# Stick-breaking attention: the second head's high parts rounded on ScalarE, both heads' weights computed back to back

## The reference, cut to what matters

```
def stick_breaking_attention(q, k, v):
...
        z = jnp.einsum('bthd,bshd->bhts', qt, k).astype(jnp.float32) * scale
        strict = s_idx[None, :] < t[:, None]
        log_beta = jax.nn.log_sigmoid(z)
        log_1mb = jnp.where(strict, log_beta - z, 0.0)
        after = lax.cumsum(log_1mb, axis=3, reverse=True) - log_1mb
        a = jnp.where(strict, jnp.exp(log_beta + after), 0.0)
        o = jnp.einsum('bhts,bshd->bthd', a.astype(v.dtype), v)
```

## Time and profile before

| what | value |
|---|---|
| runs | 658.02 us median, 657.94 to 658.09 |
| profiled execution | 658.28 us, span 656.5 us from first to last instruction |
| granted TensorE clock, mean | 0.999 |
| TensorE busy | 647.1 us, 99% of the span |
| VectorE, ScalarE, GpSimd busy | 460.2, 384.4, 163.6 us |
| chain that ended last | TensorE 93%, ScalarE 2%, VectorE 2%, GpSimd 1% |

### The profile page before, as it was taken

One profiled execution on the slowest core, in us unless ns is written; L12 is line 12 of the kernel. 1 busy time (PEld: TensorE's weight loads), 2 busy tenths in 40 slices (PEclk: granted clock), 3 DMA queues, 4 the chain that ended last, 5 costly groups with the idle time before them and its releaser, 6 DMA issues.

```text
span 656.5 us, 9977 instructions
## 1 busy us (share of the span) xinstructions
PE 647.1 (99%) x3574; PEld 539.6 (82%) x3574; DVE 460.2 (70%) x627; ACT 384.4 (59%) x561; POOL 163.6 (25%) x123
## 2 busy tenths in 40 slices
PE   9999999999999999999999999999999999999996
PEld 6888887577888888888887888777888888888885
DVE  6498766877697878786457646676678788886532
ACT  7556355866757667666345435665567676767330
POOL 0323300001053434441001000680123434343000
PEclk9999999999999999999999999999999999999999
DMA  9887633004356363637652663304255444544601
GB/s 351 335 302 282 226 129 129 1 6 189 132 199 245 136 247 128 246 138 283 231 192 73 250 249 135 129 1 189 100 182 202 180 204 165 219 147 182 247 1 64
DMA packets 18971, 115.60 MB, mean 176 GB/s; under 512 B 2911, under 2 KB 3453, under 8 KB 6013
## 3 DMA queue, kind: packets, MB, share of 16 engines
q1 hardware_dynamic: 17789, 111.52, 45.4%
q10 hardware_dynamic: 1152, 3.67, 1.6%
HBM read 114.14 MB, written 1.05 MB: 175 GB/s over the span
## 4 chain that ended last, share of the span: by engine, by line
PE 93%; ACT 2%; DVE 2%; issue 1%; POOL 1%; DVEq 0%; POOLq 0%; ACTq 0%
PE ps L1422 27%; PE ps L1429 14%; PE ps L1379 11%; PE ps L1380 11%; PE ps L1381 11%; PE ps L1451 5%; PE ps L1506 2%; PE ps L1750 1%; PE ps L1634 1%; PE ps L1370 1%; PE ps L1678 1%; PE ps L1900 1%; PE ps L1884 1%; PE ps L1600 1%; POOL sb_splo L1351 1%
## 5 line engine op out<-in xcount | busy, mean ns | idle before, releaser
L777 DVE TENSOR_TENSOR wlo<-raw,whi 128x2048 fp32r<-128x2048 f32 x99 | 226.9, 2323 | 72.8 <-ACT whi L413 72.7
L413 ACT CAST whi<-raw 128x2048 fp32r<-128x2048 f32 x99 | 185.8, 1917 | 48.8 <-PE ps L1381 42.0
L1422 PE MATMUL ps<-xpair,whi 128*128 128x512 f32 x768 | 183.3, 391 | 0.0
L1422 PEld LDWEIGHTS ps<-xpair,whi 128*128 128x128 f32 x768 | 141.2, 188 | 27.6
L1429 PEld LDWEIGHTS ps<-xpair,wlo 128*128 128x128 f32 x768 | 98.5, 191 | 3.7
L1429 PE MATMUL ps<-xpair,wlo 128*128 128x256 f32 x768 | 99.6, 283 | 0.0
L1327 POOL TENSOR_TENSOR hidf<-act_g,conv 128x512 f32<-128x512 f32 x22 | 76.0, 3455 | 85.1 <-ACT act_g L671 85.1
L1379 PE MATMUL ps<-whi,hid_hi 128*128 128x512 f32 x176 | 68.5, 389 | 0.0
L1380 PE MATMUL ps<-wlo,hid_hi 128*128 128x512 f32 x176 | 68.5, 389 | 0.0
L1381 PE MATMUL ps<-whi,hid_lo 128*128 128x512 f32 x176 | 68.5, 389 | 0.0
L1379 PE MATMUL ps<-whi,xpair 128*128 128x512 f32 x168 | 67.7, 403 | 0.1
(11 more groups left out here) (197 smaller groups left out, 789.0 us busy)
## 6 DMA issues: line engine op xcount, KB each, us to landing
raw<-in_weights SPq DMA_DIRECT2D x101, 1024.0 KB, 4.9
c_gpost<-in_gpost ACTq DMA_DIRECT2D x4, 512.0 KB, 5.7
raw<-in_weights SPq DMA_DIRECT2D x3, 512.0 KB, 6.6
c_gpre<-in_gpre ACTq DMA_DIRECT2D x3, 512.0 KB, 4.3
h<-in_x SPq DMA_DIRECT2D x2, 512.0 KB, 3.9
out<-h SPq DMA_DIRECT2D x4, 256.0 KB, 2.0
raw<-in_weights SPq DMA_DIRECT2D x2, 256.0 KB, 4.7
t<-in_masks SPq DMA_DIRECT2D x1, 512.0 KB, 12.0
```

Source lines behind the costliest of these rows:

```text
L413: act.copy(whi[:, slot, :], raw[:, slot, :]).then_inc(hi_done, 1)
L777: dve.tensor_tensor(wlo[:, slot, :], raw[:, slot, :], whi[:, slot, :].bitcast(F32), ALU.subtract).then_inc(lo_done, 1)
L1422: pe.matmul(ps[:, b0 + m, :], whi[:, slot, cols], xpair[:, kt].rearrange("p a c -> p (a c)"), start=kt == 0, stop=kt == KT - 1, skip_group ...
```

## The change

On ScalarE the two W of a pair now stand together, in front of both E. The rounding of the second head's softplus is taken from GpSimd and becomes a copy on ScalarE (`sb_second_hi`), behind the E and in front of the L; for pair 0 it stands at the end of the work beside unit 5. GpSimd keeps the first head's rounding and both low parts; its low part of the second head waits for the new semaphore `sb_sph1`. VectorE and TensorE keep their lists.

```
-        sb_z, sb_absd, sb_exp1, sb_ln, sb_spd, sb_sph, sb_spl, sb_cum, sb_prob, sb_pv, sb_ohi, sb_olo = (
-            sem("sb_" + s) for s in ("z", "absd", "exp1", "ln", "spd", "sph", "spl", "cum", "prob", "pv", "ohi", "olo"))
+        sb_z, sb_absd, sb_exp1, sb_ln, sb_spd, sb_sph, sb_sph1, sb_spl, sb_cum, sb_prob, sb_pv, sb_ohi, sb_olo = (
+            sem("sb_" + s) for s in ("z", "absd", "exp1", "ln", "spd", "sph", "sph1", "spl", "cum", "prob", "pv", "ohi", "olo"))
...
+            def sb_second_hi(n):
+                act.wait_ge(sb_spd, 2 * n + 2)
+                if n >= 2:
+                    act.wait_ge(sb_cum, 2 * (n - 2) + 2)
+                act.copy(sb_sphi[:, n % 2, 1], sb_sp[:, n % 3, 1]).then_inc(sb_sph1, 1)
+
...
                             for hd in range(2):
                                 sb_log(1, hd)
+                            sb_second_hi(0)
...
             for n in range(NP):
                 for hd in range(2):
                     sb_weights(n, hd)
-                    if n + 2 < NP:
+                if n + 2 < NP:
+                    for hd in range(2):
                         sb_exp(n + 2, hd)
                 if n == 0:
                     act.wait_ge(unit_used, ODD_END["unit", 5])
                     act.copy(vbuf[:, :, BLK:2 * BLK], ps[:, 6:8, :]).then_inc(in_free_act, 1)
+                if n + 1 < NP:
+                    sb_second_hi(n + 1)
                 if n + 2 < NP:
                     for hd in range(2):
                         sb_log(n + 2, hd)
...
-                pool.tensor_copy(sb_sphi[:, n % 2, hd], sb_sp[:, n % 3, hd]).then_inc(sb_sph, 1)
-                pool.wait_ge(sb_sph, 2 * n + hd + 1)
+                if hd == 0:
+                    pool.tensor_copy(sb_sphi[:, n % 2, hd], sb_sp[:, n % 3, hd]).then_inc(sb_sph, 1)
+                    pool.wait_ge(sb_sph, n + 1)
+                else:
+                    pool.wait_ge(sb_sph1, n + 1)
                 pool.tensor_tensor(sb_splo[:, n % 2, hd], sb_sp[:, n % 3, hd], sb_sphi[:, n % 2, hd].bitcast(F32),
                                    ALU.subtract).then_inc(sb_spl, 1)
```

## The result

The changed kernel takes 660.70 us (median of 6 runs, 660.52 to 660.94), the kernel before, run beside it, 658.15 us (6 runs, 657.94 to 658.26). The ratio is 1.0039, 95% interval [1.0029, 1.0049]: 2.6 us slower (1.9 to 3.2). The forecast was slower, 660.2 us, range 659.1 to 661.4. The profiled execution took 660.61 us with a span of 658.8 us, against 658.28 and 656.5 us before.

What follows compares the result with a forecast made beforehand. A second way through ScalarE's copy and GpSimd's low part was to set a 3.74 us period, not TensorE's 3.08; 2.2 us lost on 658.28 gives 660.5, less 0.26 for the median: 660.2 us, range 659.1 to 661.4.

Steps and rivals of the forecast that it cites:

- The way and its pieces: Loop from W(n, 1) through ScalarE's copy, GpSimd's low part and TensorE's sums to W(n+1, 1): 3.74 us a pair.
- three places to the copy: ScalarE's steps through W, E, E to the copy, 0.37 to 0.42 us each: 1.20 us.
- the hand-over to GpSimd: From the end of ScalarE's copy to the start of GpSimd's low part of head 1: 0.08 us.
- The first pairs: Start of the stick-breaking stage: W(1, 1) at 424.13 against 423.97 before, entering the periods 0.16 us late.
- The 0.2 us that the prediction put to this: By the VectorE and GpSimd port lock rule, the split and low(0, 1) end earlier: 0.2 us off the sum.
- The sum: Five periods of 3.74 us from W(1, 1) to W(6, 1): head 1's sums of pair 6 come 2.2 us late.
- the last step: Stage's last step, no E left: the second way is 2.94 us, TensorE's 3.48 us bounds, nothing more is lost.
- the last step of the sum: From the profiled execution, 660.5 us, to the median of runs, 0.26 us lower: 660.2 us.
- hidden second way: Rival: low part done before head 1's sums need it, TensorE's 3.08 us sets the period: 656.5 us; chance 0.08.
- the neutral case: Rival: second way about as long as the present period, 3.30 to 3.45 us, no change: 658.0 us; chance 0.12.
- The clock: Rival: TensorE's idle time drops its clock to the lower level in this stage: 668 us; chance 0.02.
- ScalarE's added work does not count: ScalarE's busy time with eight more copies: 2.87 us of the 3.74 us period, so it does not fall behind.

Runs made afterwards that it cites:

- the reorder alone: Kernel before the change, with both W of a pair put before both E and all roundings kept on GpSimd: 657.61 us, ratio 0.9994.
- the spare copy: Both W before both E, GpSimd keeping all roundings, plus ScalarE's copy at the change's place into a tile nobody reads: 658.81 us, ratio 1.0007 to the kernel before.
- copy-first kernel: Changed kernel with the copy for the next pair directly behind the two W, in front of the E: 657.34 us, ratio 0.9985 to the kernel before.

## Why the prediction was right

**The way and its pieces.** It named the way that would set the period and priced it at 3.74 us; it measured 3.82. Piece by piece: three places to the copy 1.20, measured 432.62 - 431.41 = 1.21; the copy 0.52, measured 0.50; ScalarE to GpSimd 0.08, measured 0.17; the low part 1.00, measured 1.01; GpSimd to TensorE 0.05, the same; the products 0.79, the same; TensorE to ScalarE 0.10, measured 0.09. The one mis-sized term is the hand-over to GpSimd, taken from a place where GpSimd waits for one semaphore only, while the new low part waits for three; with one wait it is 0.07 us here too.

**The first pairs.** W(1, 1) was forecast for 424.13 and came at 423.76. The prediction left the end of low(0, 1) at 417.17; the timeline of VectorE's split and GpSimd there, and W(1, 1), answer to the earlier trace rows:

```profile
413.61 2.29 DVE L787 TENSOR_TENSOR wlo<-raw,whi 128x2048 fp32r<-128x2048 f32 x1 [0.26 <-ACT whi L413]
...
415.79 1.01 POOL L1364 TENSOR_TENSOR sb_splo<-sb_sp,sb_sphi 128x384 fp32r<-128x384 f32 x1 [2.15 <-ACT sb_sphi L723]
...
423.76 0.49 ACT L729 ACTIVATE sb_a<-ps 128x384 f32<-128x384 f32 x1 [0.81 <-PE ps L1915]
```

The split took 2.29 us instead of 2.62, and the low part 1.01 instead of 2.93: it ended at 416.80. So this step was mis-sized by 0.37 us. Of that, 0.08 us is only that this execution reached the split earlier (413.61, not 413.69); the other 0.29 us came with the change. M(2, 0), E(2, 0), the copy of `vbuf` and the copy for pair 1 all come 0.36 to 0.38 us sooner than the prediction has them, and so does W(1, 1).

In the kernel before, GpSimd worked beside the whole split: its low part, and ahead of that high(0, 1), which started 0.04 us before the split and which the change takes away.

```profile
413.65 0.51 POOL L1349 CAST sb_sphi<-sb_sp 128x384 fp32r<-128x384 f32 x1
```

In the two experiments that keep this rounding on GpSimd, the reorder alone and the spare copy, the split took 2.61 and 2.62 us; in the other six it took 2.29 us, as in the changed kernel.

The prediction had set a rule against its own row here, the lock of the Trainium skill's "SBUF — State Buffer", section "SBUF: two separate sides". These rows agree with it: the rounding started first and the split took longer, and without the rounding it took 2.29 us. No run separates the rounding from the low part that followed it. The 0.2 us that the prediction put to this had no working; it had the right sign and was somewhat small.

**The sum.** Five periods with 0.08 us more each, 0.4 us, and a start 0.37 us earlier cancel. That was luck: the two errors have different causes. Head 1's sums of pair 6 were forecast for 441.94 and started here (TensorE's timeline, pairs 6 and 7):

```profile
442.01 0.44 PE L1913 MATMUL ps<-sb_sphi,wg_parts 128*128 128x384 f32 x1
...
445.55 0.39 PE L1913 MATMUL ps<-sb_sphi,wg_parts 128*128 128x384 f32 x1
```

That is 2.28 us behind the earlier trace rows; at pair 7 it is 445.55 - 443.21 = 2.34 us, and the span grew by 2.3 us: as forecast, the last step loses hardly anything more (0.06 us) and nothing is won back behind it. The profiled execution was forecast for 660.5 us and took 660.61. Most of the 0.5 us between the forecast of 660.2 us and the median of 660.70 us comes from the last step of the sum, which set the median 0.26 us below the profiled execution; here it lies 0.09 us above.

**The rivals.** The hidden second way and the neutral case fell with the 3.82 us. The clock did not fall; a window of 3.70 us in the middle pairs, a little shorter than the period and to be read as the earlier trace rows, has granted clock 1.00 with TensorE busy 3.17 us:

```profile
427.90:431.60 3.70, 3.17 (x28) 2.42 (x26) 2.58 (x6) 2.87 (x8) 2.33 (x4) 1.00 0.00 0
```

The statement that ScalarE's added work does not count was too simple. Its busy 2.87 us do fit into the window, and the copy-first kernel bears the same load at no loss. But the spare-copy run suggests that, with the wait gone and four pieces a pair on GpSimd, the push on both L costs up to some 0.9 us.

## What to carry to other kernels

Work moved to an idle engine is only as early as its place in that engine's list allows. Before such a move, follow the result around the loop: if what is released by it is the input of the next turn of the same loop, every instruction in front of it is paid once a turn, here 0.41 us per place. Then move the instruction to the front of the list and look for the next thing it waits for; here the place alone turned 2.6 us lost into about 1 us won, and with one wait on GpSimd and an earlier softplus it became 1.8 to 2.0 us.

## What was not expected of the hardware

With three waits in front of a GpSimd instruction, two of them satisfied before ScalarE's copy even began, ScalarE's end to GpSimd's start took 0.17 us; with one wait it was 0.07 us. The chain of the changed kernel points to the reason: there the wait for the copy (L1363, 433.15) stands ahead of that for the older sums (L1358, 433.27), although the code names them the other way round, so a satisfied wait was still gone through behind the copy. Here the other two are implied by the one that comes last, and leaving them out shortened the period from 3.82 to 434.93 - 431.20 = 3.73 us:

```profile
431.20 0.49 ACT L729 ACTIVATE sb_a<-ps 128x384 f32<-128x384 f32 x1 [0.74 <-PE ps L1915]
...
434.93 0.49 ACT L729 ACTIVATE sb_a<-ps 128x384 f32<-128x384 f32 x1 [0.72 <-PE ps L1915]
```
